# Latent attention: the scores of two heads of a query tile as one block, their rope products in the two row halves of the array

## The reference

```python
q = jnp.einsum('btc,ce->bte', cq, w_uq).reshape(B, T, MLA_HEADS, MLA_NOPE + MLA_ROPE)   # 8 heads, 128 + 64
q = jnp.concatenate([q[..., :MLA_NOPE], rope(q[..., MLA_NOPE:], pos_q)], axis=-1)
k_nope = jnp.einsum('bsc,chd->bshd', ckv_all, w_uk)
v = jnp.einsum('bsc,chd->bshd', ckv_all, w_uv)
k_rot = jnp.broadcast_to(kpe_all[:, :, None, :], k_nope.shape[:3] + (MLA_ROPE,))
k = jnp.concatenate([k_nope, k_rot], axis=-1)
o = block_attention(q, k, v, grp_q, grp_k, (MLA_NOPE + MLA_ROPE) ** -0.5)
```

## Time and profile before

| | us |
|---|---|
| median of three runs | 1208.31 |
| the three runs | 1207.9, 1208.31, 1215.74 |
| the profiled execution | 1205.93 |
| its span on the core | 1204.1 |
| TensorE busy in the span | 1110.6 |
| VectorE, ScalarE, GpSimd busy | 566.9, 260.6, 220.4 |
| first half of the latent attention | 761.0 to 813.4 |
| second half | 846.1 to 900.0 |

### The profile page before, as it was taken

The page is one execution under the profiler, slowest core; times in us unless marked ns, Lnnn a source line. Parts: engine busy times, 40 slices in busy tenths (PEclk is TensorE's granted clock), DMA queues, the critical chain, the costliest instruction groups (busy, mean ns, idle before and its releaser), DMA issues.

```text
span 1204.1 us, 18616 instructions
## 1 busy us (share of the span) xinstructions
PE 1110.6 (92%) x7460; PEld 623.9 (52%) x7466; DVE 566.9 (47%) x1351; ACT 260.6 (22%) x615; POOL 220.4 (18%) x383
## 2 busy tenths in 40 slices
PE   8998999999899969999979989999999978999995
PEld 4556776654674543333335547787784553333331
DVE  2068779710563354553457331350452354555337
ACT  0214355321440001111111222332330001111114
POOL 0015545430201211000124310000000111100123
PEclk9999999999899989999999999999999989999998
DMA  9103403253635178899787222001205167899854
GB/s 364 71 1 117 182 1 141 71 176 130 33 85 214 64 276 290 338 415 382 268 274 267 81 109 70 1 1 70 70 18 228 64 274 253 322 414 376 308 190 156
DMA packets 41976, 215.58 MB, mean 179 GB/s; under 512 B 4504, under 2 KB 6104, under 8 KB 32544
## 3 DMA queue, kind: packets, MB, share of 16 engines
q1 hardware_dynamic: 24288, 152.76, 32.8%
q0 software_dynamic: 17312, 60.80, 16.2%
q10 hardware_dynamic: 288, 0.80, 0.2%
HBM read 181.02 MB, written 33.29 MB: 178 GB/s over the span
## 4 chain that ended last, share of the span: by engine, by line
PE 78%; DVE 9%; DMA 5%; issue 4%; ACT 2%; POOL 2%; SPq 0%; DVEq 0%; POOLq 0%; ACTq 0%
PE pair L1542 13%; PE pair L1146 9%; PE pair L1426 9%; PE pair L1563 7%; PE pair L1267 5%; PE pair L1672 5%; PE pair L1345 5%; PE pair L1157 4%; PE pair L1390 3%; PE pair L1134 2%; PE pair L1528 2%; DMA arena<-x_rows,ints 2%; DMA ring<-in_even_w_in 2%; PE pair L1705 2%; PE pair L1129 1%
## 5 line engine op out<-in xcount | busy, mean ns | idle before, releaser
L1542 PE MATMUL pair<-ring,arena 128*32 128x512 f32 x608 | 128.5, 595 | 0.0
L1146 PE MATMUL pair<-ring,xT 128*128 128x512 f32 x256 | 111.3, 593 | 0.6 <-DMA ring<-in_even_w_in 0.6
L1542 PE MATMUL pair<-arena 128*32 128x512 f32 x640 | 86.4, 601 | 12.4 <-issue 8.7
L1267 PE MATMUL pair<-xT,ring 128*128 128x296 f32 x320 | 85.1, 421 | 6.9 <-ACT arena L1789 3.0
L918 POOL TENSOR_TENSOR arena<-arena 128x128 f32<-128x128 f32 x140 | 58.4, 451 | 144.9 <-PE pair L1193 78.1
L896 POOL TENSOR_SCALAR small<-small 128x1 f32<-128x1 f32 (+3 forms) x45 | 15.5, 344 | 367.3 <-DVE small L2347 317.0
L1146 PEld LDWEIGHTS pair<-ring,xT 128*128 128x128 f32 x256 | 48.1, 190 | 59.5 <-issue 57.9
L1345 PE MATMUL pair<-arena 128*128 128x264 f32 (+8 forms) x270 | 74.7, 407 | 2.8 <-ACT arena L1779 1.8
L1563 PE MATMUL pair<-ring,arena 128*32 128x512 f32 x368 | 75.4, 611 | 1.5 <-issue 1.1
L1042 POOL DMA_INDIRECT arena<-x_rows,ints x26 | 26.5, 1019 | 262.7 <-PE pair L1528 162.6
L1267 PEld LDWEIGHTS pair<-xT,ring 128*128 128x128 f32 x320 | 60.4, 193 | 25.8 <-issue 9.4
(11 more groups left out here) (388 smaller groups left out, 2048.3 us busy)
## 6 DMA issues: line engine op xcount, KB each, us to landing
ring<-in_moe_w_gate_up SPq DMA_DIRECT2D x14, 2048.0 KB, 9.9
arena<-in_moe_w_gate_up SPq DMA_DIRECT2D x12, 2048.0 KB, 11.0
ring<-in_moe_w_down SPq DMA_DIRECT2D x14, 1024.0 KB, 11.7
y_rows<-arena SPq DMA_DIRECT2D x25, 512.0 KB, 8.6
arena<-in_moe_w_down SPq DMA_DIRECT2D x12, 1024.0 KB, 9.8
xT<-in_moe_w_gate_up SPq DMA_DIRECT2D x6, 2048.0 KB, 14.2
ring<-in_even_w_in SPq DMA_DIRECT2D x5, 2048.0 KB, 7.8
y_rows<-xr POOLq DMA_DIRECT2D x13, 512.0 KB, 9.0
```

Of the source, the lines that this page charges most:

```text
L1146: last = pe.matmul(ps[0:P, 0:n], xT[:, k, 128 * i:128 * i + P], w[:, k, :], start=(k == 0), stop=(k == chunks - 1))
L1267: last = pe.matmul(ps[0:w.shape[2], 512 * s:512 * s + n], w[:, k, :], xT[:, k, n * s:n * s + n], start=(k == 0), stop=(k == KD - 1))
L1542: last = pe.matmul(bank[c, :], xgT[:, e % 2, k, c], expert_place(x)[0][:, k, :], start=(k == 0), stop=(k == KD - 1))
```

## The change

Three things. The units of a half are ordered by pairs of heads: for each pair, tiles 0 to 3, and in each tile head 2k and then 2k+1; the absorbed units stand behind tiles 1 and 3 of the first pair (and the meta unit behind tile 1 of the last). The scores of both heads are issued in one block, `two_heads_scores`, when the even head's turn comes; it claims both PSUM pairs, makes the nope products of both heads, then the rope products of each part with 64 rows each, the even head's from rows 0 to 63 and the odd head's from rows 64 to 127, and both masks. `peT` has one version, with no zeros, so that the memsets, the wait for them and one of two copies a tile are gone.

```diff
@@ -266,7 +266,7 @@
         r2 = Region()
         cqT = r2.take(4 * TOK).rearrange("p (k t) -> p k t", k=4)
         ckT = r2.take(2 * KCOL).rearrange("p (k t) -> p k t", k=2)
-        peT = r2.take(2 * KCOL).rearrange("p (v t) -> p v t", v=2)
+        peT = r2.take(KCOL)
         ckpT = r2.take(2 * PAST).rearrange("p (k t) -> p k t", k=2)
         ped = r2.take(PAST + TILES[4])
         qpT = r2.take(4 * TOK).rearrange("p (k t) -> p k t", k=4)
@@ -393,12 +393,13 @@
         MLA_AT = []
         for g in range(2):
             MLA_AT.append(len(att_units))
-            for hh in range(4):
-                att_units += [("mla", 4 * g + hh, i) for i in range(4)]
-                if hh < 2:
-                    att_units.append(("pair", 2 * g + hh, 4))
-                elif (g, hh) == (1, 2):
-                    att_units.append(("meta", 0, 4))
+            for two in range(2):
+                for i in range(4):
+                    att_units += [("mla", 4 * g + 2 * two + half, i) for half in range(2)]
+                    if two == 0 and i % 2 == 1:
+                        att_units.append(("pair", 2 * g + i // 2, 4))
+                    elif (g, two, i) == (1, 1, 1):
+                        att_units.append(("meta", 0, 4))
         MLA_AT.append(len(att_units))
         absorbed = [n for n, (kind, _, _) in enumerate(att_units) if kind in ("pair", "meta")]
         ticket(("f", 0))
@@ -580,7 +581,7 @@
         sc_sb = signal("probs_scaled", list(range(N_ATT)))
         pz_sb = signal("prompt_probs_padded", [0, 1])
         vz_sb = signal("last_value_rows_zeroed", ["fox", "mla"])
-        pez_sb = signal("rope_keys_then_paired_queries_padded", ["all", "queries"])
+        pez_sb = signal("paired_queries_padded", ["queries"])
         pT_a = signal("pT_blocks_written", [n for n in range(N_ATT) if att_units[n][0] != "meta"])
         pT_b = signal("pT_own_written", list(range(N_ATT)))
         oT_ps = signal("oT_in_psum", list(range(N_ATT)))
@@ -1320,9 +1321,6 @@
                 if kind == "fox":
                     lq, keys, past = [fq[:, h, c0:c0 + P]], [fkT[:, h, :]], [kpT[:, h, :]]
                     m_diag = const("m_causal")
-                elif kind == "mla":
-                    lq = [qnT[:, hh, c0:c0 + P], qpT[:, h // 2, c0:c0 + P]]
-                    keys, m_diag = [knT[:, hh, :], peT[:, h % 2, :]], const("m_group")
                 elif kind == "pair":
                     lq = [qa[:, c, 2 * (h % 2):2 * (h % 2) + 2, :] for c in range(2)] + [qrd[:, h, :]]
                     own = [ckT[:, 0, NM + SEQ:NM + META0], ckT[:, 1, NM + SEQ:NM + META0], ped[:, PAST:PAST + NS]]
@@ -1351,6 +1349,28 @@
                                          start=False, stop=True)
                 last.then_inc(pe_full.sem(("S", n)), 1)
 
+            def two_heads_scores(n):
+
+                _, h, i = att_units[n]
+                c0, banks = 128 * i, [claim(pe, ("S", n + v)) for v in range(2)]
+                _, parts = score_parts(n)
+                for v in range(2):
+                    done = 0
+                    for lo, cols in parts:
+                        pe.matmul(banks[v][:, lo:lo + cols], qnT[:, h % 4 + v, c0:c0 + 128],
+                                  knT[:, h % 4 + v, done:done + cols], start=True, stop=False)
+                        done += cols
+                done = 0
+                for lo, cols in parts:
+                    for v, rows in enumerate((slice(0, 64), slice(64, 128))):
+                        pe.matmul(banks[v][:, lo:lo + cols], qpT[rows, h // 2, c0:c0 + 128],
+                                  peT[rows, done:done + cols], start=False, stop=(lo != parts[-1][0]))
+                    done += cols
+                end = parts[-1][0] + parts[-1][1]
+                for v in range(2):
+                    pe.matmul(banks[v][:, end - 64:end], identb[:, :], const("m_group"), start=False, stop=True
+                              ).then_inc(pe_full.sem(("S", n + v)), 1)
+
             def att_transpose(n):
 
                 nb, P, k0 = att_rows(n)
@@ -1392,8 +1412,10 @@
 
             def attention(first, last):
                 for n in range(first, last + 3):
-                    if n < last:
+                    if n < last and att_units[n][0] != "mla":
                         att_scores(n)
+                    elif n < last and att_units[n][1] % 2 == 0:
+                        two_heads_scores(n)
                     if first <= n - 2 < last:
                         att_transpose(n - 2)
                     if n - 3 >= first:
@@ -2005,14 +2027,9 @@
                 copy(ckT[:, :, NM + 128 * j:NM + 128 * j + P], latent[:, :, 0:P])
                 if j == 4:
                     copy(ckT[:, :, 0:NM], latent[:, :, NS:P])
-                if j == 0:
-                    act.wait_ge(*pez_sb["all"])
-                for v in range(2):
-                    half = slice(64 * v, 64 * v + 64)
-                    if j == 4:
-                        copy(peT[half, v, 0:NM], ps[half, 768 + NS:768 + P])
-                    last = copy(peT[half, v, NM + 128 * j:NM + 128 * j + P], ps[half, 768:768 + P])
+                last = copy(peT[:, NM + 128 * j:NM + 128 * j + P], ps[:, 768:768 + P])
                 if j == 4:
+                    copy(peT[:, 0:NM], ps[:, 768 + NS:768 + P])
                     last = copy(ped[:, PAST:], ps[:, 768:768 + P])
                 last.then_inc(ps_free.sem(("mt", j)), 1)
 
@@ -2673,9 +2690,6 @@
                     combined_norm(i + 2)
                 if i + 3 < NT:
                     combined_stats(i + 3)
-                if i == 0:
-                    dve.memset(peT[64:128, 0, :], 0.0)
-                    dve.memset(peT[0:64, 1, :], 0.0).then_inc(pez_sb.sem, 1)
                 latents(i)
             dve.wait_ge(*mi_sb[NT - 1])
             for i in range(NT):
```

## The result

The changed kernel takes 1241.08 us in the median of four runs (1236.22 to 1246.32); the kernel before, beside it, 1209.13. The ratio is 1.0245 [1.0212, 1.0279]; the ratios here are estimated from the single runs and differ a little from the quotients of the medians (1.0264 here). In a second measurement, beside 21 runs of the kernel before, it was 1.0204 [1.0166, 1.0242]. The sign of the forecast holds, and so does its mechanism but for the clock. The time does not: 1241 is 14 us above the 1227 forecast and 2 above the top of the range.

What follows compares the result with a forecast made beforehand. TensorE was taken to bound the kernel. Two halves, waits less row-half savings, +19.5 us, hidden copies lost at their starts +1.2, rope-key copies -0.6: +20.1, giving 1226, stated as 1227 us; range 1217 to 1239 for 8 in 10.

Steps and rivals of the forecast that it cites:

- The sign of the forecast: Whole kernel: slower by over 1%, above 1220 us, given 85%.
- The row halves overlap: Rope products of two heads on TensorE run fully at once, saving 9.1 us of columns over four pairs of heads.
- rival 1: Rope products in the two row halves do not overlap: the 9.1 us come back, 1236 us; chance 13%.
- the switch: Changing TensorE's array shape: 0.19 us to the halves, 0.12 back, over 16 groups 5.0 us.
- (a): First transposes wait for the output copy of an earlier unit, 8 times a half instead of 2: +3.6 us a half.
- (b): Next block of scores waits for the second exponential: 7.2 us a half, before 0.2, so +7.0.
- (c): At a half's start both PSUM pairs are claimed first, so copies of absorbed queries are no longer hidden: +1.2 us in all.
- the restarts: TensorE's weight load showing after each wait, 0.10 us on products and 0.03 on transposes: +0.7 us a half.
- Interleaving costs nothing with single scores: Interleaving two heads changes which unit sizes meet; with single scores that order costs 0.
- The copies of the rope keys: Keys' rope part written by one copy instead of two: 0.17 + 0.12 us in the last tile, -0.6 us with tile 3.
- rival 2: TensorE's granted clock falls in the halves, likely at the 2.4 us gap at each start: 1230 to 1235 us; chance 10%.
- Rival 3: TensorE's own work hides the new waits, leaving only -4.2 and -0.6 us: 1203 us; chance 11%.

Runs made afterwards that it cites:

- single halves: Kernel before, order and single scores kept, each head's rope products on its own 64 rows with one copy of the rope keys: 1218.80 us, ratio 1.0068.
- filled version: Changed kernel plus ten unread bf16 products of 512 columns behind the first block of each half: 1228.43 us, ratio 1.0146.
- late claim on the changed kernel: Changed kernel with transposes of the other key blocks issued ahead of the wait for the output copy, own block's behind it: 1228.06 us, ratio 1.0113.
- rope first: Changed kernel without the block: both heads' rope products made with the even head's scores, odd head's nope products and mask one unit later: 1211.04 us, ratio 0.9996.
- kernel before with the late claim: Kernel before with only the transposes of the key blocks moved ahead of the wait for the output copy: 1204.11 us, ratio 0.9975.

## Why the forecast was right in kind and short in size

**TensorE is what bounds.** Right: 78% of the chain before and after, while VectorE and ScalarE do as much in the halves as before (28.57 and 19.57 us).

**The row halves overlap; rival 1 is wrong.** 0.87 us for four records of 400 columns is 0.68 at full overlap and 0.19 for the switch, as the forecast put both. Rival 1 would have shown 1.35 + 0.19. In the block of 528 keys, where four pairs of 264 columns follow each other, the second pair starts 0.22 us ahead of the third and the third 0.22 ahead of the fourth (starts of the single records), and one full-row record of that length takes 0.22 too (eight in 1.79). At the full clock the scores of two heads, from the first record to the first transpose behind the masks, take 1.17, 1.82, 2.46 and 3.11 us for 144, 272, 400 and 528 keys, and 1.11, 1.96, 2.82 and 3.69 in the block without row halves. That is 1.02 us over the four tiles, 2.0 a half, with 2.1 forecast; each group pays 0.31 to 0.32 us for its switches, as put. At 144 keys the packing loses 0.06 us.

The Trainium skill (TensorE: Matmul & The Clock Gate, Part 3: Packing small matmuls, Measured speedup vs the span model) gives four row tiles as 3.07 times as fast. No run here has four row tiles; two halves in f32 reach the full factor of two inside a group, by the 0.22 us above. The Trainium skill (TensorEngine Tiling (Array Packing), Key Properties) says that changing the tiling mode drains TensorE. The trace agrees in that every change costs time: 0.31 us a group here, and 0.36 there and back in the single halves.

**The waits (a), (b), (c).** Right in kind. The filled version shows them at the full clock: halves 10.3 and 10.0 us longer, 20.3 together, where the forecast had 19.5 + 1.2 = 20.7. By kind: (a) 16 gaps of some 0.5 us as put, though the kernel before had lost 1.3 us a half to its two, not 1.8; (b) 11.8 us of gaps in the changed kernel in 12 pieces, forecast 14.4 us in 14 pieces: the largest 2.4 (measured 2.2), the next 1.1 (1.03), and every other one smaller than put or not there; (c) the first scores of the halves waited 1.17 and 1.07 us, where the seconds had waited some 0.45 before, so +1.3 for +1.2. The total agrees better than its terms, and that is luck: what (b) had too much, the restarts had too little. Four records with 400 keys behind a gap take 1.58 us of the filled version's chain (first line), and 1.34 in the kernel before where none is ahead (second line):

```profile
776.84 1.58 PE pair L1360 x4
861.87 1.34 PE pair L1345 x4
```

So a restart of products cost 0.24 us and not the 0.10 of the forecast, 2.9 us over the 12 gaps of (b).

**Interleaving costs nothing with single scores.** Right, to 0.02 us a half.

**The copies of the rope keys.** Right where it can be seen. The chain of waits of after at the last latent tile, answering:

```profile
729.49 0.42 ACT arena L2025
729.92 0.19 ACT arena L2027
730.11 0.09 ACT arena L2029
730.20 0.13 ACT arena L2030
730.33 0.08 ACT arena L2032
730.41 0.14 ACT arena L2033
730.55 0.14 issue
```

From the first copy to the issue 1.06 us. The same stretch before was 1.43 us (720.85 to 722.28): 0.37 less, where 0.29 was put. The other 0.3 us of the forecast, of tile 3, is not shown.

**The clock, rival 2: the step that failed.** The place was named (the gap of 2.4 us at each half's start) and so was the price (two to six falls of 1.25 us, 2.5 to 7.5 us); the chance, 10%, was wrong. The clock fell in both halves of both profiles of the changed kernel, and cost 5.75 us in the first (3.7 + 2.05) and 7.3 in the second (3.6 + 3.7). The forecast had put this term at nothing, on a stretch of 5 us with TensorE busy for 3.02 that kept the clock; and it had priced one fall at 1.25 us, since half of the 5 us of the other stretch there were low. Here it stayed at 1.2 GHz for 6.8 and 10.2 us, and one fall cost 2.05 to 3.7. I also weighed the 2.4 us gap alone, though the new gap (c) stands right ahead of it: 1.17 and 2.22 us idle with 1.3 us of products between. That it takes both is my reading and not shown: filling the second kept the clock up, so the first alone does not bring it down, but no run has the second alone.

**The rest of the 14 us.** 20.3 us at the full clock and 5.75 or 7.3 of clock are the +26.1 and +27.6 that the halves measured. With the copies that is a time of about 1208 + 27 - 0.6 = 1235 us, and by the second ratio 1208.31 x 1.0204 = 1233. The first median of 1241 lies above that, and its profiled execution shows where: 8.3 us ahead of the first half, which the second profile does not repeat in full, and 3.5 us behind the second. **Open:** both profiles of the changed kernel spend 307.7 and 308.5 us behind the halves, in code that is unchanged, where the before profile has 304.1 and the block with full rows and the filled one 302.2 and 301.8. Both show a fall of the clock for 6.8 us some 272 us behind the halves. The kernel before, the block with full rows and the filled one have none there, while the late claim on the changed kernel and both versions of rope first without fillers have one of 3.4 us. Whether that comes from the changed kernel's timing or from chance, two profiles do not tell.

**Open too:** why the clock was low for only 3.4 us a half in the block with full rows, with the same gaps at its start and a first block that is the same to 0.06 us. There the fall set in 7.1 us behind the half's start, in all four halves of the changed kernel 4.8 to 5.0 us behind it. The late claim on the changed kernel had one of each: 5.0 us and then low for 10.2, 7.0 us and then low for 3.4. So it may be the moment of the fall that sets its length, and not the form of the rope products; no run varied that alone, and the moment does not say it all, since of the four early falls of the changed kernel one lasted 6.8 us and three 10.2.

**Rival 3, the waits are hidden.** Wrong for the change as made. Rope first comes near it: leave one head's scores at the odd unit's turn and 1211 us comes out beside 1213, ratio 0.9996, though not the 4.8 us of gain that the rival had.

## What to carry to other kernels

Before you issue two units' scores as one block, write down what then stands between the end of the block and the next one: scores are not only work, they are the cover of the previous unit's softmax, and here some 12 us of waits a half stand against 2 us won (4.6 us of columns less 2.5 of switches), a loss of 10 at the full clock. A product that can be made early without its partner (here the rope part, which may start the odd head's sum) gives the packing without giving up the cover. When a change opens gaps, look for neighbouring ones before you put the clock at nothing, and if they cannot be closed, try to fill them with products nobody reads; here that gave back 5.75 us.

## What the hardware showed that I had not expected

- Behind a gap of 1.17 us (1.07 in the second halves), 1.3 us of products and a gap of 2.22 us the granted clock fell from 1.00 to 0.50 (2.4 to 1.2 GHz) in eight of eight such starts of a half, for 3.4 to 10.2 us; with the second gap filled by bf16 products it stayed at 1.00 in both. With gaps of 0.8 and some 0.5 us (rope first, without and with the late claim) it fell in three of four halves, for 3.4 to 6.8 us.
- It did not return when the gap ended: from 772.5 to 782.7 us TensorE was busy for 8.48 of 10.20 us, and stayed at 0.50.
- Two 64-row halves in f32 run fully at once, both writing all 128 output partitions into different PSUM pairs: their records start 6 or 7 ns apart, and a pair of 264 columns takes 0.22 us, as one full-row record does.
- A bank of a PSUM pair can be written by transposes while VectorE reads the pair's other bank. In the tail of the first half of the kernel before with the late claim, four transposes run from 811.65 to 812.31 us and the output copy from the same pair from 811.72 to 812.00, and each half is 1.0 us shorter.
